# The norms' scales by Ln and Exp from one table set, loaded by hand, and the high passes first at the last norm

## The reference

```python
a = modulate(rmsnorm(x, g_pre), mod[0], mod[1])             # norm "x"
x = x + mod[2] * rmsnorm(short_gated_conv(a), g_post)       # chain "post"
f = squared_relu_mlp(modulate(rmsnorm(x, g_pre_ff), mod[3], mod[4]))
x = x + mod[5] * rmsnorm(f, g_post_ff)                      # chain "post_ff"

z = rms_norm(x, ln1_g) @ w_in                               # stage z_in
y_a = (gelu(u) * spatial_gating(layer_norm(gelu(v)))) @ w_a_out
y_b = silu(layer_norm(conv31(p * sigmoid(g_lin)))) @ w_b_out
y_c = stick_breaking_attention(rms_norm(q), rms_norm(k), vv) @ w_c_out
x = x + (sigmoid gates * (y_a, y_b, y_c), summed) @ w_out   # branch, mix_out
up = conv3(rms_norm(x, ln2_g) @ w_up)                       # norm "ln2", stage up
x = x + (silu(gate) * val) @ w_down
```

## Time and profile before

| | |
|---|---|
| median of 3 runs | 830.81 us (829.1 to 830.86) |
| the profiled execution | 831.66 us, its span 829.9 us |
| PE busy | 755.5 us (91%) |
| PE weight loads busy | 716.0 us (86%) |
| DVE busy | 564.0 us (68%) |
| ACT busy | 422.2 us (51%) |
| POOL busy | 14.5 us (2%) |
| mean granted clock of TensorE | 0.961 |
| bytes moved | 152.13 MB, 183 GB/s |

### The profile page before, as it was taken

One profiled execution on the slowest core, in us unless ns is written; L12 is line 12 of the kernel. 1 busy time (PEld: TensorE's weight loads), 2 busy tenths in 40 slices (PEclk: granted clock), 3 DMA queues, 4 the chain that ended last, 5 costly groups with the idle time before them and its releaser, 6 DMA issues.

```text
span 829.9 us, 13700 instructions
## 1 busy us (share of the span) xinstructions
PE 755.5 (91%) x5496; PEld 716.0 (86%) x5496; DVE 564.0 (68%) x738; ACT 422.2 (51%) x488; POOL 14.5 (2%) x28
## 2 busy tenths in 40 slices
PE   5379999599999999949999999898997999999998
PEld 4379988499999888849987989788997999999998
DVE  5978887376556744425879977754966888887441
ACT  3324344664555332386496656666545555554330
POOL 1000000000000000020000100000000000000000
PEclk9598998889999999988999999999999999999999
DMA  9688896235556885423534424333761545533540
GB/s 377 254 280 282 284 364 247 101 130 176 202 159 196 299 276 186 153 111 105 208 146 159 146 102 152 114 99 107 248 243 62 195 166 190 190 123 133 185 155 26
DMA packets 38652, 152.13 MB, mean 183 GB/s; under 512 B 2704, under 2 KB 19216, under 8 KB 27216
## 3 DMA queue, kind: packets, MB, share of 16 engines
q1 hardware_dynamic: 38240, 150.20, 52.0%
q0 software_dynamic: 368, 1.31, 0.5%
HBM read 150.45 MB, written 1.05 MB: 183 GB/s over the span
## 4 chain that ended last, share of the span: by engine, by line
PE 66%; DVE 15%; ACT 9%; DMA 6%; issue 3%; SPq 0%; DVEq 0%; POOL 0%; ACTq 0%; POOLq 0%
PE ps L1159 15%; PE ps L1161 15%; PE ps L1160 15%; DVE w_lo L736 5%; DMA raw<-in_w_sc_in 4%; PE ps L1268 4%; PE ps L1269 4%; PE ps L1270 4%; DVE ada_acc L740 3%; ACT w_hi L439 2%; PE ps L1286 1%; ACT L522 1%; DVE cacc L993 1%; ACT L523 1%; DMA raw<-in_ada 1%
## 5 line engine op out<-in xcount | busy, mean ns | idle before, releaser
L1159 PE MATMUL ps<-a_hi,w_hi 128*128 128x256 f32 x1184 | 340.2, 287 | 14.4 <-DVE sc_y L900 7.4
L736 DVE TENSOR_TENSOR w_lo<-raw,w_hi 128x2048 fp32r<-128x2048 f32 (+2 forms) x128 | 269.3, 2106 | 111.7 <-ACT w_hi L439 111.3
L1161 PE MATMUL ps<-a_hi,w_lo 128*128 128x256 f32 x1184 | 337.1, 285 | 0.0
L1160 PE MATMUL ps<-a_lo,w_hi 128*128 128x256 f32 x1184 | 336.3, 284 | 0.0
L439 ACT ACTIVATE w_hi<-raw 128x2048 fp32r<-128x2048 f32 (+2 forms) x128 | 225.2, 1763 | 138.1 <-PE ps L1270 54.3
L1159 PEld LDWEIGHTS ps<-a_hi,w_hi 128*128 128x128 f32 x1184 | 226.2, 191 | 17.3 <-issue 16.3
L1160 PEld LDWEIGHTS ps<-a_lo,w_hi 128*128 128x128 f32 x1184 | 227.2, 192 | 0.6 <-issue 0.5
L1161 PEld LDWEIGHTS ps<-a_hi,w_lo 128*128 128x128 f32 x1184 | 225.9, 191 | 0.0
L712 ACT ACTIVATE up_u<-ps,par 128x256 f32<-128x256 f32 x44 | 22.5, 561 | 57.7 <-PE ps L1161 57.7
L1268 PE MATMUL ps<-w_hi,hid_hi 128*128 128x512 f32 x128 | 50.9, 398 | 0.0
L740 DVE SCALAR_TENSOR_TENSOR ada_acc<-raw,silu_c,ada_acc 128x1024 f32<-128x1024 f32 x37 | 47.5, 1283 | 5.0 <-DMA raw<-in_ada 2.8
(11 more groups left out here) (219 smaller groups left out, 879.5 us busy)
## 6 DMA issues: line engine op xcount, KB each, us to landing
raw<-in_w_z_in SPq DMA_DIRECT2D x26, 1024.0 KB, 4.7
raw<-in_w_up SPq DMA_DIRECT2D x22, 1024.0 KB, 4.7
raw<-in_ada SPq DMA_DIRECT2D x16, 1024.0 KB, 7.0
raw<-in_w_mlp_in SPq DMA_DIRECT2D x16, 1024.0 KB, 4.7
raw<-in_w_mlp_out SPq DMA_DIRECT2D x16, 1024.0 KB, 5.8
raw<-in_w_sc_in SPq DMA_DIRECT2D x16, 768.0 KB, 5.7
raw<-in_w_down SPq DMA_DIRECT2D x16, 704.0 KB, 4.0
raw<-in_ada_half SPq DMA_DIRECT2D x16, 512.0 KB, 5.5
```

The source lines that it names most:

```text
L736: e.tensor_tensor(w_lo[:, slot, 0:words], raw[:, unit_slot, 0:words], w_hi[:, slot, 0:words].bitcast(f32), SUB).then_inc(raw_used, 1)
L1159: e.matmul(dst, w_hi[:, slot, cols], hi, start=start, stop=False, skip_group_check=skip)
L1160: e.matmul(dst, w_hi[:, slot, cols], lo, start=False, stop=False, skip_group_check=skip)
L1161: return e.matmul(dst, w_lo[:, slot, cols], hi, start=False, stop=stop, skip_group_check=skip)
```

## The change

All rstd are now a Ln and an Exp. The Sqrt of the norms x and ln2 and the reciprocals of DVE are gone. ACT loads the set `natural_log_exp_and_others` at four places: behind the Silu at the start, behind the last Sigmoid of the convolution's gates, behind the last Gelu, and behind the last `mix_high` of the branch stage. At ln2 DVE makes all eight `y` and then all eight `a_lo`, and the first block of up is `hi_first`.

```diff
@@ inverse_rms on ACT
                 r = rstd[:, number % 2, 0:width]
-                if count == D:
-                    e.activation(r, ps[:, STAT, 0:width], ACT.Sqrt, bias=eps[:, :], scale=1.0 / count).then_inc(rstd_ready, 1)
-                    return
                 ch.link(e.activation(r, ps[:, STAT, 0:width], ACT.Ln, bias=eps[:, :], scale=1.0 / count))
                 e.activation(r, r, ACT.Exp, scale=-0.5).then_inc(rstd_ready, 1)
@@ ACT's list
             e.activation(silu_c[:, :], pcol("c", 0, 8), ACT.Silu).then_inc(c_ready, 1)
+            e.preload_act_table_set("natural_log_exp_and_others")
...
                     e.activation(sig[:, i % 2, :], ps[:, bank, T:2 * T], ACT.Sigmoid).then_inc(sig_ready, 1)
+                    if i == 3:
+                        e.preload_act_table_set("natural_log_exp_and_others")
...
                                  ACT.Gelu_apprx_tanh).then_inc(z_free_act, 1)
+                    if i == 1:
+                        e.preload_act_table_set("natural_log_exp_and_others")
...
             mix_high(N_BLOCKS["branch"] - 1)
+            e.preload_act_table_set("natural_log_exp_and_others")
@@ inverse_rms on DVE
-                r = rstd[:, number % 2, 0:width]
-                if number not in range(STATN["qk"], STATN["cv"] + 1):
-                    ch.link(e.reciprocal(r, r))
-                return r
+                return rstd[:, number % 2, 0:width]
@@ normalise on DVE
-                    if i >= 2:
-                        low_part(norm, i - 2, shift)
-                low_part(norm, DT - 2, shift)
-                low_part(norm, DT - 1, shift)
+                for i in range(DT):
+                    low_part(norm, i, shift)
@@ PE, first block of up
-                    first_block(act_lo, ACT_TILE["ln2"], raw_unit(g0) + 1, g0, 0, a_hi, a_lo)
+                    hi_first(ACT_TILE["ln2"], raw_unit(g0) + 1, g0, a_hi, a_lo)
```

## The result

The change makes the kernel faster: 801.6 us, median of four runs (800.1 to 804.3), against 830.26 (829.1 to 830.86) for the kernel before in the same comparison, a ratio of 0.966 with a 95% interval of 0.963 to 0.969. The prediction was 800.5, in a range of 796 to 806.5. The profiled execution of the changed kernel took 804.3 us, the slowest of its four; 802.6 of it are span, where the kernel before had 829.9. Unrounded the two traces that are compared here differ by 27.4 us (829.95 and 802.59). Over the three comparisons made later the medians lie 28.1, 29.8 and 30.9 us apart, here 28.7.

A forecast was written before the change was run, and what follows sets the result against it. TensorE was taken to bound the kernel, with waits at the norms and attention steps. Terms of 1.7 + 6.4 + 12.0 + 6.55 + 3.6 = 30.3 us off the median of 830.81 gave 800.5 us, range 796 to 806.5.

The forecast's parts named there:

- Term 1: First norm: VectorE's reciprocal goes and the gain survives the short convolution stage; 1.7 us.
- they follow DVE: Short convolution stage: weight loads are issued when DVE releases a buffer, so the first norm's 1.7 us survive.
- Term 2: Chain "post": first token half 0.5 us, second half 5.0 us, shorter half clock 0.9 us; 6.4 us in all.
- Term 3: Chain "post_ff": second turn 9.4 us earlier, full clock there worth 2.65 us; 12.0 us in all.
- Term 4: z_in: layer norm and attention waits shrink by 4.9 us, clock adds 1.65 us; 6.55 us in all.
- the ring: z_in attention: ACT and DVE's 16.58 us loop takes 15.3 with one load less; three rounds give 3.8 us.
- Term 5: Last norm, ln2: reciprocal 1.4 us, start on high parts 0.7 us, clock 1.5 us; 3.6 us in all.
- Less survives: Rival: DMA eats the first norm's 1.7 us and the clock falls in shorter waits too; 809 us; chance 0.12.
- More: Rival: clock stays full in "post", behind single-column sums (6.5 and 3.4 us stretches) or in its wait; 794 us; chance 0.07.
- It does not do what it says: Rival: the chip still loads a table at each pair; 829 to 831 us, no change; chance 0.015.
- Slower: Rival: closer work keeps TensorE at half rate in z_in; all 105 us would cost 52, 853 us; chance 0.015.

The follow-up runs named there:

- set_only: Kernel before plus explicit loads of the shared table set at three places; roots, reciprocals and last norm's order unchanged: 806.73 us, ratio 0.971 to the kernel before.
- recip4_x: Changed kernel plus four unread reciprocals of 256 columns on VectorE behind the first norm: 808.96 us.
- recip_x: Changed kernel plus one unread reciprocal of 256 columns on VectorE behind the first norm: 803.3 us.
- loads_post_ff: Changed kernel plus eight reloads of the resident table set, ahead of each Ln and Exp of the chain post_ff: 814.69 us, ratio 0.981 to the kernel before.
- loads_att: Changed kernel plus eight table reloads in z_in's attention steps, ahead of each second softplus Ln and each Exp of the weights: 807.05 us.
- ln2_old: Changed kernel with the old order of high and low parts at the last norm, without the reciprocal: 804.07 us.
- fill_post: Changed kernel plus 16 unread matmuls in TensorE's wait ahead of the second turn of the chain post: 800.79 us.
- fill_both: Changed kernel plus unread matmuls: 16 ahead of post's second turn and 7 ahead of the third branch block: 799.64 us.
- fill_all: Changed kernel plus unread matmuls: 16 ahead of post's second turn, 7 ahead of the third branch block, 8 ahead of the first up block: 799.94 us.

## Why the prediction was right, step by step

**Term 1** (1.7 predicted). Right at its own place, 1.4 us at the first matmul of sc_in: the reciprocal's 1.74 went, VectorE's products had started 0.2 later. Of this 0.2 was left at sc_out in the first pair of traces. Most of the loss stands at two waits of TensorE, 0.71 us instead of 0.23 at 100.4 us and 0.94 instead of 0.37 ahead of sc_out, behind ScalarE's waits for weights. The argument "they follow DVE" does not hold there: it was read from a DMA share of 0.56 at 36 us, while the share is 0.93 from 96 to 120, and ScalarE waited for these weights 13 times in the kernel before. I had looked at the beginning of the stage and not at the rest of it. Whether the loss is a rule or this pair's luck is open: the spread of B, 2.4 us, is larger than the term, and the runs of set_only and recip4_x speak for a start that is kept.

**Term 2** (6.4 predicted, 6.2 in this trace). The first half gave 0.57 (0.5), the wait became 4.7 (4.85), so 5.1 instead of 5.0 there. The half clock behind the restart lasted 4.1 us, where I took 3.4; with 5.2 before, that is worth about 0.5 instead of 0.9. The lower bound of 1.7 stands on no row; in the ten traces whose second turn waits 4.74 us the full clock came back 3.0 to 6.2 us behind the restart. The other traces' C puts this stage's gain at 6.2 to 8.2: how long the clock stays low from 126 to 170 us differs by run (what it lacks there sums up to 5.1 us in recip_x, 8.5 in the trace of after). No run puts back the loads of this chain alone; set_only shows that the shared set is enough for its two waits.

**Term 3** (12.0 predicted, 12.2). No wait ahead of the first turn, 1.17 ahead of the second (1.5), full clock, turn of 2.05 us. loads_post_ff gives the waits back to 0.02 us, and D with them: shown.

**Term 4** (6.55 predicted, 6.7). 1.23 of the layer norm gone and a wait of 0.50 at the sum over cacc, as forecast; loads_att gives back 3.9 of the ring (3.8) and 1.6 of clock (1.65): shown.

**Term 5** (3.6 predicted, 3.6). 2.14 us behind the last sum (2.1), clock full; parts of 1.4, 0.7 and 1.5 each measured by set_only and ln2_old: shown. But its 1.5 of clock is not certain for this code: in fill_post and fill_both the clock fell behind the same 2.14 us, and G was 1.8 and 1.5 longer.

**What no term had**: 1.4 us lost to the half clock in the branch stage. It stood among the rivals ("Less survives"), where I argued against it with the two short waits at the branch that had left the clock full. The same two waits, 1.31 and 1.93 us, are in the changed kernel, and behind them it fell. It did so in all kernels without fillers but loads_post_ff and loads_att, where a fall of the old kernel had come back at 359 or at 512; why it falls behind the one wait or the other is open. What is left of the forecast's 30.3 is 27.4 in the traces: 1.5 for term 1 and 1.4 for this make up the difference. The medians, 830.26 and 801.6, are 28.7 apart, since the profiled run of the changed kernel is the slowest of its four. The four comparisons of medians lie at 28.1 to 30.9 us, 29.4 in the mean, so the sum of 30.3 was too large by about 1 us. That the time missed by 1.1 us in this comparison, and not by the 2.9 of its traces, is luck.

The other rivals: "More" did not come, though C in recip_x and ln2_old lies 1.6 to 2 us toward it; the first of its two stretches at half rate was 6.9 us long in the kernel before and not 6.5. "It does not do what it says" is out by the 10 loads. "Slower" is out: z_in's attention ran at full clock, but fill_post and fill_all show that it can fall there for 3 to 4 us. Its price was too small: work of 105 us at full clock lasts 105 us longer at half rate, not 52, if TensorE bounds all of it.

## What to carry to other kernels

Count table loads on the chain that the bounding engine waits for and not on ScalarE as a whole: the same eight loads cost 13 us in one chain, 5.5 in a ring and 0.4 beside matmuls (12.4, 3.9 and 0.4 by the length of the stage). Where two functions that alternate are in one set, load that set explicitly ahead of the chain, in a wait that is there anyway, and look at every wait behind it for the clock as well as for its length. A gain ahead of a stage that is fed by transfers should be followed to the end of that stage before it is counted.

## What the runs showed of the hardware that I had not expected

A load of the table set that is resident is not skipped: 1283 ns each, mean of eight, and 0.02 us to the next instruction.

The granted clock falls to 1.2 GHz behind a wait as short as 1.65 us in one trace and stays full behind a wait of the same length in another, with the same instructions around both: at 462 us in fill_post and fill_all but not in fill_both, at 604 us in fill_post and fill_both but not in the changed kernel. The Trainium skill ("TensorE: Matmul & The Clock Gate", Part 1) says that activity is looked at on a clock that does not start with the kernel; the prediction said that no run showed this yet. These traces agree with it in that the place of a fall moves between kernels whose work there is the same and starts some us earlier or later; they do not show what the chip looks at. And the kernel's spread of 4 us from run to run (799.99 to 804.56 over both comparisons) is as large as what B (2.4 us) and C (2.0 us) together differ by between traces.
